# Hyena long convolution: the spectral products in re-im batches straight from PSUM, their sums and the turned remainder on VectorE instead of GpSimd

## The reference, cut to what matters

```python
z = v
for o, gate in enumerate((x1, x2)):
    zf = jnp.fft.rfft(z, n=2 * L, axis=1)
    conv = jnp.fft.irfft(zf * resp[None, :, o], n=2 * L, axis=1)[:, :L]
    z = gate * (conv + z * bias[o])
return z.astype(h.dtype) @ lp['w_out']
```

## Time and profile before

| | before |
|---|---|
| median of 3 runs | 4929.57 us |
| the profiled execution, first to last instruction (its own time as used here) | 4928.7 us |
| PE busy | 4195.4 us (85%) |
| DVE busy | 2588.4 us (53%) |
| ACT busy | 1114.1 us (23%) |
| POOL busy | 1204.1 us (24%) |
| mean granted TensorE clock | 0.915 of full speed |

### The profile page before, as it was taken

How to read it: one execution, slowest core, us unless ns; L and a number is a source line. 1 busy time by engine, 2 the same in 40 slices (tenths; PEclk the granted TensorE clock), 3 DMA queues, 4 the chain that set the end, 5 groups by cost and what they waited for, 6 DMA issues and landing times.

```text
span 4928.7 us, 50705 instructions
## 1 busy us (share of the span) xinstructions
PE 4195.4 (85%) x21688; PEld 3482.8 (71%) x21688; DVE 2588.4 (53%) x2823; ACT 1114.1 (23%) x1417; POOL 1204.1 (24%) x674
## 2 busy tenths in 40 slices
PE   6599887888688999999778889876554889999998
PEld 2288777777477888888656777765554778888886
DVE  6758055555316444444375545548885164444443
ACT  5435112222113111111232332311111131111112
POOL 0321133333133222222320000012221332222224
PEclk9799799999799999999888888887887999999999
DMA  8421000000210111111112122132211101111111
GB/s 326 181 67 34 37 1 1 1 1 1 86 33 26 39 39 39 36 39 40 64 52 67 59 89 75 57 137 79 79 66 73 30 28 39 39 39 36 39 40 60
DMA packets 253816, 280.42 MB, mean 57 GB/s; under 512 B 7941, under 2 KB 217814, under 8 KB 249079
## 3 DMA queue, kind: packets, MB, share of 16 engines
q1 hardware_dynamic: 253592, 277.18, 16.9%
HBM read 219.48 MB, written 57.67 MB: 56 GB/s over the span
## 4 chain that ended last, share of the span: by engine, by line
PE 72%; DVE 18%; ACT 3%; issue 3%; POOL 2%; DMA 1%; SPq 0%; POOLq 0%; DVEq 0%; ACTq 0%
PE PS L606 51%; DVE piece L1481 7%; PE PS L1549 7%; DVE piece L1035 3%; PE PS L1006 2%; PE PS L1007 2%; DVE piece L532 2%; PE PS L1719 2%; PE PS L1002 2%; PE PS L410 1%; DVE piece L426 1%; PE PS L718 1%; ACT piece L394 1%; DVE piece L525 1%; POOL piece L546 1%
## 5 line engine op out<-in xcount | busy, mean ns | idle before, releaser
L606 PE MATMUL PS<-piece,piece 128*128 128x512 f32 (+1 forms) x13824 | 2756.1, 361 | 162.8 <-POOL piece L550 100.3
L606 PEld LDWEIGHTS PS<-piece,piece 128*128 128x128 f32 x13824 | 2313.2, 191 | 608.5 <-issue 152.6
L589 POOL TENSOR_TENSOR piece<-piece,piece 128x1024 fp32r<-128x1024 f32 (+1 forms) x204 | 499.8, 2451 | 2414.8 <-ACT piece L583 2414.8
L1549 PE MATMUL PS<-piece,piece 128*128 128x256 f32 x1920 | 437.9, 390 | 138.9 <-DVE piece L1481 90.2
L1422 DVE SCALAR_TENSOR_TENSOR piece<-piece,piece,piece 128x1024 f32<-128x1024 f32 x352 | 534.9, 1520 | 12.6
L1549 PEld LDWEIGHTS PS<-piece,piece 128*128 128x128 f32 x1920 | 372.7, 196 | 201.4 <-issue 127.8
L1442 DVE SCALAR_TENSOR_TENSOR piece<-PS,piece,piece 128x1024 f32<-128x1024 f32 x224 | 187.8, 880 | 415.7 <-PE PS L606 415.7
L583 ACT ACTIVATE piece<-piece 128x1024 fp32r<-128x1024 f32 (+1 forms) x204 | 205.0, 1006 | 675.8 <-PE PS L606 635.3
L1035 DVE TENSOR_TENSOR piece<-piece,PS 128x512 f32<-128x512 f32 x288 | 185.4, 684 | 250.4 <-PE PS L1007 193.0
L1419 DVE TENSOR_SCALAR piece<-piece,piece 128x1024 f32<-128x1024 f32 x44 | 35.8, 813 | 482.3 <-ACT piece L1383 482.3
L1481 DVE TENSOR_TENSOR piece<-piece 128x512 f32<-128x512 f32 (+2 forms) x168 | 163.2, 971 | 87.5 <-ACT piece L1969 68.2
(11 more groups left out here) (212 smaller groups left out, 4034.3 us busy)
## 6 DMA issues: line engine op xcount, KB each, us to landing
piece<-in_l_ada_w SPq DMA_DIRECT2D x24, 2048.0 KB, 10.1
piece<-in_l_ffn_up SPq DMA_DIRECT2D x88, 512.0 KB, 3.7
piece<-in_l_w_in SPq DMA_DIRECT2D x44, 512.0 KB, 5.5
piece<-in_l_ffn_down SPq DMA_DIRECT2D x48, 384.0 KB, 3.0
filters_s<-piece SPq DMA_DIRECT2D x8, 2176.0 KB, 6.6
piece<-filters_s SPq DMA_DIRECT2D x8, 2176.0 KB, 8.0
hyena_tokens<-piece SPq DMA_DIRECT2D x24, 640.0 KB, 4.5
piece<-hyena_tokens SPq DMA_DIRECT2D x12, 1280.0 KB, 5.5
```

The lines of the kernel that those rows point to most:

```text
L589: eng.tensor_tensor(LO[i % 2][0][:, 0:n], RAW[i % 2][:, 0:n], HI[i % 2][1][:, 0:n], ALU.subtract)\
L606: m = eng.matmul(PS[:, bank + b, 0:n], w, x[:, a:a + n], start=first and n_ == 0, stop=last and n_ == 2)
L1549: m = eng.matmul(PS[:, bank, o * HC:(o + 1) * HC], M[i][o], rhs[i], start=i == 0, stop=i == 1)
```

## The change

The four products per leaf become two, each twice as wide: VectorE multiplies the whole bank (re and im together) by the filter's real part (`near`) and by its imaginary part (`cross`), the filter row being read twice through a broadcast. From leaf 2 of group s on, two banks go in one instruction (128x1024). The sums of two leaves are made by one subtraction and one addition (128x2x256) on VectorE itself, right behind their products. The remainder of the turned result is subtracted on VectorE straight out of PSUM (`spread`), so TURNED, ScalarE's full copies and GpSimd's program of this stage are gone. The diff, cut:

```diff
+            BATCH = {"s": ((0, 1), (1, 1), (2, 2), (4, 2), (6, 2)), "p": ((0, 1), (1, 1))}
...
                 def inverse(g, l):
                     wait_conv_bank(eng, g, rnd, "i", l)
-                    eng.wait_ge(poC[g].sem, poC[g].at(f"b{l}", rnd))
+                    eng.wait_ge(veC[g].sem, veC[g].at(f"im{l - l % 2}", rnd))
...
                     if rnd and order == 0:
-                        eng.wait_ge(acO.sem, acO.at("all1", c - 1))
+                        eng.wait_ge(veO.sem, veO.at("lo1", c - 1))
...
                             eng.activation(HH[:, 2 * c + half, :], psum(3 * half, N), ACT.Copy).then_inc(*acO.did(f"hi{half}", c))
-                            if half:
-                                eng.wait_ge(poO.sem, poO.at("lo0", c))
-                            elif c:
-                                eng.wait_ge(poO.sem, poO.at("lo1", c - 1))
-                            eng.activation(TURNED, psum(3 * half, N), ACT.Copy).then_inc(*acO.did(f"all{half}", c))
...
+                        eng.wait_ge(peC[g].sem, peC[g].at(f"z{l + n - 1}", rnd))
+                        eng.tensor_tensor(keep, both, near, ALU.mult).then_inc(*ve.did(f"near{l}", rnd))
+                        eng.tensor_tensor(other, both, cross, ALU.mult).then_inc(*ve.did(f"cross{l}", rnd))
+                        if (l + n) % 2 == 0:
...
+                            eng.wait_ge(ve.sem, ve.at(f"cross{l}", rnd))
+                            eng.tensor_tensor(kr, kr, ti, ALU.subtract).then_inc(*ve.did(f"re{a}", rnd))
+                            eng.tensor_tensor(ki, ki, tr, ALU.add).then_inc(*ve.did(f"im{a}", rnd))
+
+                def spread(c):
+
+                    for half in range(2):
+                        eng.wait_ge(acO.sem, acO.at(f"hi{half}", c))
+                        eng.tensor_tensor(HL[:, 2 * c + half, :], psum(3 * half, N), HH32[:, 2 * c + half, :], ALU.subtract).then_inc(*veO.did(f"lo{half}", c))
...
                     gate("s", f"it{N_INV - 1}", 1.0)
+                    if order:
+                        spread(c)
```

More of the change, by code:

```diff
@@ L1472, in pair, with ends @@
             return v.rearrange("p u v c -> p u (v c)")
+        def ends(ap, last):
+            v = ap[:, 0:last + 1, :]
+            return v.rearrange("p (u v) c -> p u v c", v=last + 1).to_broadcast([P, 1, last + 1, HC])[:, :, 0:last + 1:last, :]
         def chain(eng, st, tag, rnd):
@@ L1875, in last_leaf, with taken @@
                 return LEAVES[g][-1]
+            def taken(g, l):
+                return f"cross{max(a for a, n in BATCH[g] if a <= l)}"
             def bank_of(g, kind, l):
@@ L1885, in wait_conv_bank @@
                     m = item - len(LEAVES[g])
-                    who, what = (veC[g], f"done{item}") if m < 0 else (acC[g], f"i{m}")
+                    who, what = (veC[g], taken(g, item)) if m < 0 else (acC[g], f"i{m}")
                     eng.wait_ge(who.sem, who.at(what, rnd))
@@ L1909, in _ @@
                         if rnd + 1 < nj:
[L1910 removed]
+                            eng.wait_ge(veC[g].sem, veC[g].at(taken(g, last_leaf(g)), rnd))
                             eng.dma_start(HB[g], filt_dram[g][rnd + 1]).then_inc(s_h[g], 16)
@@ L2001, in multiply @@
                     eng.wait_ge(s_h[g], 16 * (rnd + 1))
[L2002 removed]
+                    for l, n in BATCH[g]:
                         bank = bank_of(g, "z", l)
[L2004 to L2007, removed]
[L2008 to L2010 removed]
+                        both = PS[:, bank:bank + n, :].rearrange("p n (u c) -> p n u c", u=2)
+                        keep, other = (X[:, 2 * l:2 * (l + n), :].rearrange("p (n u) c -> p n u c", u=2) for X in (K, T))
+                        if l == 0:
+                            edge = 2 * len(LEAVES[g])
+                            near = ends(H, edge)
+                        else:
+                            near = H[:, 2 * l:2 * (l + n), :].rearrange("p (n u) c -> p n u c", u=2)[:, :, 0:1, :].to_broadcast([P, n, 2, HC])
+                        cross = H[:, 2 * l:2 * (l + n), :].rearrange("p (n u) c -> p n u c", u=2)[:, :, 1:2, :].to_broadcast([P, n, 2, HC])
+                        eng.wait_ge(peC[g].sem, peC[g].at(f"z{l + n - 1}", rnd))
+                        eng.tensor_tensor(keep, both, near, ALU.mult).then_inc(*ve.did(f"near{l}", rnd))
+                        eng.tensor_tensor(other, both, cross, ALU.mult).then_inc(*ve.did(f"cross{l}", rnd))
+                        if (l + n) % 2 == 0:
+                            a = l + n - 2
+                            kr, ki, tr, ti = (X[:, 2 * a:2 * a + 4, :].rearrange("p (n u) c -> p n u c", u=2)[:, :, u, :] for X in (K, T) for u in range(2))
+                            eng.wait_ge(ve.sem, ve.at(f"cross{l}", rnd))
+                            eng.tensor_tensor(kr, kr, ti, ALU.subtract).then_inc(*ve.did(f"re{a}", rnd))
+                            eng.tensor_tensor(ki, ki, tr, ALU.add).then_inc(*ve.did(f"im{a}", rnd))
@@ L2033, in _ @@
                     gate("s", f"it{N_INV - 1}", 1.0)
-            done = [peO, acO, poO] + [x[g] for x in (peC, acC, veC, poC) for g in "sp"]
+                    if order:
+                        spread(c)
+            done = [peO, acO, veO] + [x[g] for x in (peC, acC, veC) for g in "sp"]
             x_ready, part3 = project(A["l1_w_out"], done, done, 1, (s_x, 32))
```

27 lines of the change are left out of this document (6 added, 21 removed).

## The result

The changed kernel takes 4945.73 us (median of 5 runs, 4941.44 to 4950.53) where the kernel before takes 4929.57 (5 runs, 4924.16 to 4930.85): ratio 1.0039, 95% interval 1.0026 to 1.0051. Run again beside another set of runs of the kernel before it gave 1.0029 (1.0019 to 1.0040). It is slower by 14 to 19 us; 4947 had been forecast.

The account below looks back on a forecast made before the run. It took the chain tree, first sums, 12 leaves, untree as the bound, above all how late p's first sum is ready. First sums 6.2, turn 6.0, end -1.0 and clock 6.8 gave +18.0 us: 4947, range 4937 to 4958 (about 0.83).

Parts of the forecast that it names:

- What bounds the stage: Convolution rounds: tree, first sums, 12 leaves, untree form the chain; in seven of eight rounds p's first sum counts.
- A: First sums of p, on VectorE: PE restarts 0.88 us later in seven rounds, 6.2 us slower (4.6 to 9.1).
- The lower bound: First sums of p: six instructions 0.6 us apart without a wait, restart later by 0.65 us, 4.6 in all.
- No hold inside the 12 leaves: PE's 12 leaves: last products read 17.0 us after the tree, ninth leaf at 17.9, so PE isn't held.
- B: Turn at a chunk's end, three times: tree begins 7.1 us later, 5.15 us of stretching goes, net 6.0 us slower.
- C: End of the stage: weights issued 4.6 us earlier but queued behind the x_spill read, so a gain of 1.0 us.
- The rival in which the end pays: End of the stage: first weights land 4.6 us earlier, as issued; total 4937 us, chance 0.10.
- D: PE's clock after pauses of 2.3 to 3.1 us: four falls in seven, 1.7 us each, 6.8 us slower (0 to 12).
- the rival with all seven: PE's clock falls in every one of the seven pauses ahead of the 12 leaves, 11.9 us; total 4957, chance 0.14.
- the theory of four separate terms: Convolution stage, stated for the experiments: first sums, turn, clock and an end giving nothing separately make the 18.4 us.
- the rival: Convolution stage, stated for the experiments: first sums, turn or clock only shadows another; undoing one takes all or nothing; no chance given.
- The sum: Whole span: 6.2 + 6.0 - 1.0 + 6.8 = +18.0 us, giving 4947.

Follow-up runs that it names:

- second experiment: Changed kernel with group p back to 256-wide products and its sums on GpSimd, s still changed: ratio 1.0008 to the kernel before.
- tenth experiment: Changed kernel with p's products and sums inside the tree, remainders in the next tree, weights first, s's sums on VectorE, GpSimd empty: ratio 0.9980 to the kernel before.
- fifth experiment: Changed kernel with the remainder back on GpSimd and ScalarE's full copies, products and sums still changed: ratio 1.0023 to the kernel before.
- first experiment: Changed kernel with a turn's two remainders moved into the next chunk's tree, still on VectorE: ratio 1.0006 to the kernel before.
- fourth experiment: Changed kernel with the x_spill read issued behind the first two weight tiles of the output projection: ratio 1.0030 to the kernel before.
- eighth experiment: Kernel before with one more 256-wide GpSimd subtraction ahead of its first sum of p, result unread: ratio 1.0008 to the kernel before.
- ninth experiment: Kernel before with three more 256-wide GpSimd subtractions ahead of its first sum of p, results unread: ratio 1.0067 to the kernel before.

## Why the prediction was right, point by point

**What bounds the stage.** The chain tree, first sums, 12 leaves, untree held: each of the four terms was found on it, and the page's shares moved by a point at most.

**A, first sums.** Restart 3.96 us behind the first product, forecast 3.93; before 3.05. Seven times 0.91 is 6.4 us, forecast 6.2. (The lower bound leaves out the 0.13 us to PE; with it, it is some 0.8 us a round and 5.4 in all.) The second experiment took it away. The Trainium skill, "VectorE: DVE Perf Modes", section "The DRAIN you can't avoid", has the next operation wait until the one in front has left the pipe, and in the same place excepts one that nothing holds; without the exception A would have been 9.1 by the prediction's estimate. The products here start 0.60 apart and last 0.68, so for these rows the exception is what applies.

**No hold inside the 12 leaves.** Right: the runs at full clock last the 20.96 us of before. The last product ends at 3371.18 + 1.22 = 3372.40, 17.0 us behind the tree, as worked out, and the ninth leaf starts near 3359.37 + 8 x 1.75 = 3373.4. The tenth experiment shows how thin the cover is: with p out of the way PE comes earlier, and waits.

**B, the turn.** The tree begins 7.37, 7.01 and 6.87 us behind its gate, mean 7.1 as forecast, and gets back the 5.15 us of GpSimd's hindrance. Net 8.15 us of the three turns, less A in them (2.7), is 5.4 against 6.0. The fifth experiment measured 5.4. That the order matters more than the engine the prediction did not see: in the first experiment the remainders stay on VectorE, and the three turns take 13.2 us less.

**C, the end.** Forecast a gain of 1.0, measured none: the weights were issued 5.2 us earlier behind the gate and came at the same time. The mechanism, the queue behind the x_spill read, was right, and the fourth experiment showed its size, 6.4 us. The rival in which the end pays fell with it.

**D, the clock.** Four cold bursts of 1.7 us were forecast, and four of 1.68 to 1.69 came, 6.7 us, in both profiles of the changed kernel in the same rounds. The size, read from two slices, was well founded; the count was met by luck. The step took the 2.07 us pause at the turn as the sign that pauses of 2.3 to 3.1 lose the clock often; the eighth experiment had pauses up to 2.89 and lost it nowhere. In the changed kernel five pauses were 3.13, of which two fell and three held; the other two, 1.93 and 1.99, lie below the range that the step named, and both fell, behind 48 passes that stayed at half clock for longer than in the other rounds (13.62 and 13.55 us instead of 12.40). The fourth kernel, with the same programs of PE and VectorE in the stage, has three falls, in other rounds. In the second experiment one of six pauses of 2.22 to 2.23 fell, after a turn. Over all traces here no pause under 1.9 us ahead of the 12 leaves lost the clock, and each of 1.9 us or more behind 48 passes of 13.4 us or more did (eight of eight: two in each profile of the changed kernel and in the first and the ninth). So longer pauses cost clock, as the ninth experiment shows, and which round pays depends on more than the pause, it seems on what PE did ahead of it; what the full rule is stays open. The Trainium skill, "TensorE: Matmul & The Clock Gate", section "HAM oscillation", tells of a kernel in which a wait ahead of every burst is long enough to let every burst start cold. Here it was not every burst: with 3.13 us three of five kept the full clock, so the rival with all seven did not come, and even 3.4 to 4.5 us left two of seven.

The clock is not a term of its own, as the theory of four separate terms had it: undoing A alone left one cold burst of four, and undoing B alone, or the order of the turn, left two. To that extent the rival was right.

**The sum.** 6.4 + 5.4 + 6.7 = 18.5 for a stage that grew by 18.4. The forecast's 18.0 had B 0.6 higher and took off 1.0 for an end that gave nothing, two errors that partly cancel. The span grew by 15.2 only, as the stage began 1.5 us earlier and what follows it took 1.7 less, both in the scatter. The medians differ by 16.2.

## What to carry to other kernels

Where an engine looks empty, ask whether its work lies beside something longer before moving it: GpSimd's sums of s held PE up nowhere in the kernel before, while the two places in which the receiving VectorE stands on the chain, ahead of PE's restart and behind the gate, cost 6.4 and 5.4 us, and the half clock that followed another 6.7. Work whose inputs are ready should stand ahead of the point at which other engines wait, as the remainders and p inside the tree did: for the remainders the order was worth 13.2 us in three turns, the engine 5.4. An earlier issue counts only if nothing large stands ahead of it on the same queue.

## What the hardware showed that I had not expected

A pause of PE can cost more than its length: 2.3 us more in seven rounds of the kernel before brought 12.2 us of half clock on top of 16.1. One pause lost 1.68 us in some runs and 2.9 to 3.0 in others (fifth and ninth experiments). The four cold bursts are no chance of one execution: the two profiles of the changed kernel have the same seven lengths, in the same order. Yet the fourth kernel, with the same programs of PE and VectorE in the stage, has three in other rounds, so something beyond these programs has a part in it, which no run here settles. And a 5120 KB read took 15.4 us and swallowed whole a 5.2 us earlier issue of the weights behind it.
